# Choosing experts over three tiles in turn, and splitting the first weighted-sum block before the scores end

## The reference, cut to what matters

```python
s = jnp.einsum('thzd,hzkd->thzk', qry, sub_keys)           # t tokens, h 8 heads, z 2 halves, k 128 keys
top_s, top_i = lax.top_k(s, PEER_TOPK)                     # 16 of 128, for each half
cand_s = (top_s[:, :, 0, :, None] + top_s[:, :, 1, None, :]).reshape(nt, PEER_HEADS, kk)
best_s, best_pos = lax.top_k(cand_s, PEER_TOPK)            # 16 of 256 sums
idx = jnp.take_along_axis(cand_i, best_pos, axis=-1)
gate = jax.nn.softmax(best_s, axis=-1)
...
act = jax.nn.gelu(jnp.einsum('td,thkd->thk', tb, expert_u[ib]), approximate=False)
wts = act * gb
out = jnp.einsum('thk,thkd->td', wts, expert_v[ib])
```

## Time and profile before

| | us |
|---|---|
| median of 3 runs (lowest, highest) | 2340.74 (2338.66, 2343.03) |
| the profiled execution | 2343.86 |
| its span, first to last instruction | 2342.0 |
| PE busy in it | 2259.8 (96%) |
| DVE, ACT, POOL busy | 1512.5, 902.6, 1157.2 |

### The profile page before, as it was taken

How to read it: one execution, slowest core, us unless ns; L and a number is a source line. 1 busy time by engine, 2 the same in 40 slices (tenths; PEclk the granted TensorE clock), 3 DMA queues, 4 the chain that set the end, 5 groups by cost and what they waited for, 6 DMA issues and landing times.

```text
span 2342.0 us, 30967 instructions
## 1 busy us (share of the span) xinstructions
PE 2259.8 (96%) x10852; PEld 1879.7 (80%) x10852; DVE 1512.5 (65%) x3525; ACT 902.6 (39%) x1425; POOL 1157.2 (49%) x947
## 2 busy tenths in 40 slices
PE   8999899899989999999999999999989999999998
PEld 6787688788878888888887888888877888888885
DVE  4554666677665354058887888882238888888783
ACT  6454555344334333233333333342223333323342
POOL 3433232766634333315666656665656665555610
PEclk9999999999999999999999999999999999999999
DMA  4222011232344333224444444446458999999940
GB/s 167 90 74 88 19 46 46 93 115 86 134 170 167 111 106 120 72 86 142 149 141 147 136 149 148 148 136 247 146 177 337 387 374 347 362 349 344 364 180 37
DMA packets 160321, 394.71 MB, mean 169 GB/s; under 512 B 27376, under 2 KB 93168, under 8 KB 149872
## 3 DMA queue, kind: packets, MB, share of 16 engines
q1 hardware_dynamic: 125424, 326.32, 40.0%
q0 software_dynamic: 34816, 67.41, 7.8%
HBM read 328.45 MB, written 65.21 MB: 168 GB/s over the span
## 4 chain that ended last, share of the span: by engine, by line
PE 41%; POOL 15%; issue 9%; DVE 2%; DMA 2%; ACT 1%; DVEq 0%; POOLq 0%; SPq 0%
POOL g_dense L1892 14%; PE ps L1329 13%; PE ps L2346 7%; PE ps L2347 7%; PE ps L2348 7%; PE ps L180 2%; PE ps L182 2%; PE ps L181 2%; DMA g_dense<-up_gates_summed_sb,up_gate_at_sb 1%; PE ps L1663 1%; PE ps L2398 1%; DMA expert_rows_sb<-expert_v,chosen_expert_sb 0%; POOL down_picked_gelu_sb L2099 0%; DVE up_spare_sb L1832 0%; DVE up_u_low_sb L1748 0%
## 5 line engine op out<-in xcount | busy, mean ns | idle before, releaser
L1892 POOL DMA_INDIRECT g_dense<-up_gates_summed_sb,up_gate_at_sb x384 | 418.5, 1090 | 308.2 <-issue 232.1
L180 PE MATMUL ps<-n_high_sb,up_u_high_sb 128*128 128x512 f32 x1024 | 398.6, 389 | 0.8 <-issue 0.8
L182 PE MATMUL ps<-n_high_sb,up_u_low_sb 128*128 128x512 f32 x1024 | 398.4, 389 | 0.1
L181 PE MATMUL ps<-n_low_sb,up_u_high_sb 128*128 128x512 f32 x1024 | 398.4, 389 | 0.0
L2346 PE MATMUL ps<-down_v_high_sb,down_w_high_sb 128*128 128x512 f32 x768 | 301.3, 392 | 12.3 <-issue 7.5
L2347 PE MATMUL ps<-down_v_low_sb,down_w_high_sb 128*128 128x512 f32 x768 | 300.8, 392 | 0.0
L2348 PE MATMUL ps<-down_v_high_sb,down_w_low_sb 128*128 128x512 f32 x768 | 300.5, 391 | 0.0
L1748 DVE TENSOR_TENSOR up_u_low_sb<-up_u_sb,up_u_high_sb 128x1024 fp32r<-128x1024 f32 x128 | 156.5, 1223 | 161.5 <-ACT up_u_high_sb L1913 140.9
L2273 ACT ACTIVATE down_v_high_sb<-down_v_sb 128x1024 fp32r<-128x1024 f32 x120 | 126.0, 1050 | 312.1 <-PE ps L2348 289.0
L1925 ACT ACTIVATE up_gelu_sb<-ps 128x512 f32<-128x512 f32 x128 | 76.6, 598 | 398.0 <-PE ps L182 282.5
L180 PEld LDWEIGHTS ps<-n_high_sb,up_u_high_sb 128*128 128x128 f32 x1024 | 192.2, 188 | 42.1 <-issue 2.0
(11 more groups left out here) (347 smaller groups left out, 4687.3 us busy)
## 6 DMA issues: line engine op xcount, KB each, us to landing
up_u_sb<-expert_u SPq DMA_DIRECT2D x128, 512.0 KB
down_v_sb<-expert_v SPq DMA_DIRECT2D x32, 2048.0 KB
a_dense<-up_gelu_sb SPq DMA_DIRECT2D x128, 256.0 KB
g_dense<-nought_sb SPq DMA_DIRECT2D x8, 3072.0 KB, 10.8
down_gelu_sb<-a_dense SPq DMA_DIRECT2D x32, 768.0 KB
down_gates_sb<-g_dense SPq DMA_DIRECT2D x32, 768.0 KB
w_slots_sb<-w_conv SPq DMA_DIRECT2D x19, 1024.0 KB, 4.8
query_slots_sb<-peer_query SPq DMA_DIRECT2D x8, 1024.0 KB, 6.1
```

Of the source, the lines that this page charges most:

```text
L180: pe.matmul(out, ah, bh, start=k == 0, stop=False)
L181: pe.matmul(out, ah, bl, start=False, stop=False)
L182: last = pe.matmul(out, al, bh, start=False, stop=k == n - 1)
L1892: pool.indirect_dma_start(cells, at, summed[:, tt, k:k + 1], None).then_inc(stored[tt], 16)
```

## The change

1. **Order of selection.** `ORDER` goes over the units first and the dense tiles inside: unit 0 of tiles 0, 1 and 2, then unit 1 of each, and so on; tile 3 last, as before. `gates` and `at_f` get a buffer per tile. POOL scatters in that order, with the second head of a unit put one unit later.
2. **Block 0 of the weighted sum.** The value pieces are copied at j = 112 to 115 and their low parts taken one by one from key 116; SP waits for all scatters in step 119 (`GATES_AT`) instead of 124 and loads block 0's gates there, block 1's in step 121; DVE makes the weights after low part 125, ACT copies them at j = 123 and 124, DVE takes their low parts after low part 127.
3. **Block 2.** SP loads its values in step 124 and its gelus and gates in step 126, and block 3 right after the score stage; the loop starts two blocks later.
4. **Rows ahead of picks.** POOL gathers the rows of block 0 when all products are made, and the picks after the `a_dense` stores; from block 1 on the order is as before.

```diff
-    WEIGHTS_AT = PEER_K - 4
-    VALUES_AT = PEER_K - 8
+    VALUES_AT = PEER_K - 16
+    GATES_AT = PEER_K - 9
+    WEIGHED_AT = PEER_K - 3
+    WEIGHTS_AT = PEER_K - 5
     UK = UNIT * TOPK
+    ORDER = [(tt, n) for n in range(UNITS) for tt in range(DENSE)] + [(tt, n) for tt in range(DENSE, TT) for n in range(UNITS)]
...
-        for tt in range(TT):
-            if tt:
+        for c, (tt, n) in enumerate(ORDER):
+            if tt and n == 0:
                 dve.wait_ge(query.out_act, 4 * tt)
...
         for n in range(split[0], PEER_K):
             low_part()
-        dve.wait_ge(low, PEER_K)
-        opening.value_lows(dve)
-        opening.weights(dve)
+            if VALUES_AT + RING <= n < VALUES_AT + RING + DOWN_J - 1:
+                opening.value_low(dve, n - VALUES_AT - RING)
+            if n == PEER_K - RING:
+                dve.wait_ge(low, n + 1)
+                opening.value_low(dve, DOWN_J - 1)
+            if n == WEIGHED_AT:
+                opening.weigh(dve)
+        opening.weight_lows(dve)
...
-            if j == WEIGHTS_AT:
+            if j == GATES_AT:
                 for tt in range(DENSE):
                     sp.wait_ge(stored[tt], 16 * HK)
                 down.load_gates(sp, 0, 0)
+            if j == GATES_AT + 2:
+                down.load_gates(sp, 1, 1)
+            if j == PEER_K - 4:
+                sp.wait_ge(opening.v_low, DOWN_J)
+                down.load_v(sp, 2, 0)
             if j == PEER_K - 2:
-                down.load_gates(sp, 1, 1)
+                sp.wait_ge(opening.w_low, DOWN_J)
+                down.load_gelus(sp, 2, 0)
+                down.load_gates(sp, 2, 0)
...
-        for h in range(5):
-            scatter(0, h)
-        for h in range(3):
-            scatter(0, 5 + h)
-            scatter(1, h)
-        scatter(1, 3)
-        for h in range(4):
-            scatter(1, 4 + h)
-            scatter(2, h)
-        for h in range(4, PEER_H):
-            scatter(2, h)
+        for c in range(DENSE * UNITS):
+            scatter(c, 0)
+            if c < 2:
+                scatter(c, 1)
+            if c > 2:
+                scatter(c - 1, 1)
+        scatter(DENSE * UNITS - 1, 1)
...
-            if j == PEER_K - 2:
+            if j in (WEIGHTS_AT, WEIGHTS_AT + 1):
                 for n in range(DOWN_J // 2):
-                    opening.weight_high(act, n)
+                    opening.weight_high(act, (j - WEIGHTS_AT) * (DOWN_J // 2) + n)
...
-            with sp.Fori(1, NB // 2) as i:
+            sp.wait_ge(w_low, 2 * JB)
+            down.load_gelus(sp, 3, 1)
+            down.load_gates(sp, 3, 1)
+            sp.wait_ge(v_low, 2 * JB)
+            down.load_v(sp, 3, 1)
+            with sp.Fori(2, NB // 2) as i:
...
             pool.wait_ge(up.prod, PEER_K)
+            rows(0)
             for x in up.a_stored:
                 pool.wait_ge(x, up.all_blocks)
-            for n in range(NB):
-                gather(n)
+            picks(0)
+            for n in range(1, NB):
+                picks(n)
+                rows(n)
```

More of the change, by code:

```diff
@@ new lines, in vector @@
+            h0, h1 = n * UNIT, (n + 1) * UNIT
+            ks, gs = slice(h0 * TOPK, h1 * TOPK), slice(h0 * G, h1 * G)
+            for hz in range(2 * h0, 2 * h1):
+                last = top16(scores[:, hz, :], spare[:, hz * PEER_K:(hz + 1) * PEER_K], top_v[:, hz, :], top_i[:, hz, :], 1.7)
+            st.done(last)
+            dve.tensor_copy(top_f[:, 2 * h0:2 * h1, :], top_i[:, 2 * h0:2 * h1, :])
+            tv, tf = (x[:, 2 * h0:2 * h1, :].rearrange("p (h z) k -> p h z k", z=2) for x in (top_v, top_f))
@@ new lines, in vector @@
+            gate = heads(gates_of(tt, n))
+            dve.tensor_tensor(gate, best[:, h0:h1, :], top1, ALU.subtract).then_inc(maxed, 1)
+            exp_at.append(split[0])
+            for z in range(2):
+                if z == 0:
+                    st.done(dve.tensor_scalar(part[:, ks], flat(pos[:, h0:h1, :]), 4, None, ALU.logical_shift_right))
+                else:
+                    st.done(dve.tensor_scalar(part[:, ks], flat(pos[:, h0:h1, :]), 15, None, ALU.bitwise_and))
+                st.done(dve.tensor_copy(part_f[:, ks], part[:, ks]))
+                eq = spare[:, gs].rearrange("p (n a) -> p n a", a=TOPK)
+                st.done(dve.tensor_tensor(eq, part_f[:, ks].unsqueeze(2).broadcast_to([P, UK, TOPK]),
+                                          iota[:, 0:TOPK].unsqueeze(1).broadcast_to([P, UK, TOPK]), ALU.is_equal))
+                st.done(dve.tensor_tensor(grid(spare[:, gs]), grid(spare[:, gs]),
+                                          tf[:, :, z, :].unsqueeze(2).broadcast_to([P, UNIT, TOPK, TOPK]), ALU.mult))
+                st.done(dve.tensor_reduce(chosen[:, z, ks], eq, AX.X, ALU.add))
+                spent(2.8)
@@ new lines, in vector @@
+            spent(1.5)
+            if tt < DENSE:
+                dve.tensor_copy(place[:, tt, ks], at_f[:, ks])
+                for h in range(h0, h1):
+                    before = slice(0, (h + 1) * TOPK)
+                    for q in range(TOPK):
+                        k = h * TOPK + q
+                        last = dve.scalar_tensor_tensor(spare[:, q * HK:q * HK + (h + 1) * TOPK], at_f[:, before], at_f[:, k:k + 1],
+                                                        gates[:, tt, before], ALU.is_equal, ALU.mult, accum_out=summed[:, tt, k:k + 1])
+                        if q % 8 == 7:
+                            spent(2.6)
+                    last.then_inc(placed, 1)
+                    dve.wait_ge(placed, c * UNIT + (h - h0) + 1)
+            else:
+                dve.tensor_copy(m.a_at[:, tt - DENSE, ks], at_f[:, ks])
+                st.done(dve.scalar_tensor_tensor(part_f[:, ks], first, float(PEER_K), second, ALU.mult, ALU.add))
+                dve.tensor_copy(m.v_row[:, tt - DENSE, ks], part_f[:, ks]).then_inc(selected, 1)
@@ L1884, in gpsimd, with scatter @@
     def gpsimd(pool):
-        def scatter(tt, h):
-            pool.wait_ge(placed, tt * PEER_H + h + 1)
+        def scatter(c, half):
+            tt, n = ORDER[c]
+            h = n * UNIT + half
+            pool.wait_ge(placed, c * UNIT + half + 1)
             if h:
@@ L2093, in _, with picks @@
         def _(pool):
-            def gather(n):
+            def picks(n):
                 for u in range(PICK):
@@ L2260, in _ @@
             up.scalar(act)
-            for j in range(JB // 2, JB):
-                opening.weight_high(act, j)
             act.wait_ge(v_in[1], 16)
```

98 lines of the change are left out of this document (30 added, 68 removed).

## The result

| | before | changed |
|---|---|---|
| median (lowest, highest), us | 2340.93 (2338.66, 2343.03) | 2324.97 (2323.33, 2328.43) |
| runs | 4 | 4 |
| the profiled execution | 2343.86 | 2328.43 |
| its span | 2342.0 | 2326.7 |

The changed kernel takes 0.9937 of the time of before, 95% interval 0.9921 to 0.9953: 16.0 us less by the medians, 15.4 by the two profiled executions. The forecast was 2333.4 in a range of 2324 to 2347.

The account below looks back on a forecast made before the run. PE, busy 96% of the span, was taken as the bound. Of 17.6 us winnable in gaps and clock, 8.8 were lost before product 124 and 1.5 at block 2: 7.3 us won, 2333.4 from the median 2340.74, range 2324 to 2347.

Parts of the forecast that it names:

- the gaps at the seam and at block 2: PE idle 7.54 us between scores and weighted sum and 4.72 us before block 2; 17.6 us winnable with the lower clock.
- the scatters that end before 1699.8: Rival, chance 0.10: POOL's transfers get shorter while SP stands still, so the gain is 16 us, time 2324.7.
- 1713.3 - T: The change's total gain in us as a function of the scatters' end, the whole 16 to 17.6 if that is below 1699.8.
- T: End of POOL's scatters, when the memset after them follows; forecast at 1706 us.
- the clock: PE's matmuls run at a lower clock level after a gap; forecast to cost 2.6 us after the idle before product 124.
- (a): Pricing POOL's removed scatter waits one by one: 9 x 2.4 = 21 us, so the memset comes at about 1708.
- (b): Pricing POOL's scatters by heads: 22 x 27.0 + 2 x 29.5 = 653 us, an end at about 1702.
- The rival in which the pauses grow as the waits go: POOL's removed scatter waits return as longer pauses: only 5 us won, scatters end at 1724, time 2351.4; chance 0.15.
- T + 8.5: Start of PE's product 124, behind the delayed load, split and low part: 1714.5, which leaves PE idle 6.2 us.
- no gap before product 124: Sign that the prediction is wrong; it expected PE to be idle there for about 6 us.
- The first gap: PE's idle time between the last score product and the weighted sum, forecast won whole: 9.9 us (7.54 + 2.4).
- The rival in which POOL's gathers wait for DVE: Row gathers wait for DVE's run of subtractions, block 2 is 4.0 + 2.6 us late, time 2338.5; chance 0.13.

Follow-up runs that it names:

- the one trace with 21: The kernel before with its 24 heads scattered tile by tile, so that 21 wait for the head issued right before: 2356.56 us, ratio 1.0058.
- the second copy: The changed kernel measured once more without an edit, beside later kernels: 2327.36 us, ratio to before 0.9944; its profiled execution took 2336.71 us.

## Why the prediction was right, and where it was off

**The direction and the cause held.** The prediction put the gaps at the seam and at block 2 on one chain of scatters. The order alone makes the gain, and without it parts 2 to 4 together win nothing. The size was off: the median, 2324.97, lies 1 us inside the stated range and 3 below the forecast's own range of 2328 to 2341. It is the number of a rival with a chance of 0.10, the scatters that end before 1699.8, 2324.7. In the profiled execution they ended 0.75 us after that. The 1713.3 - T of the sum gives 12.8 for T = 1700.55, and the rest of the 15.4 are the clock, block 2 and 0.2 us of part 2, as told below.

**Part 1.** T was taken as 1706, between (a) 1708 and (b) 1702; it came at 1700.55, and its mean over nine traces is 1701.0. Way (b), by heads, gave 653 us for the 24 heads, and they took 652.2. The mean of the chain over the nine is 651.5. The 2.5 us for a wait holds over the whole range of 2 to 21 waits, though not evenly: 3.1 for each of the first nine, 2.0 for each of the last ten. The rival in which the pauses grow as the waits go is refuted both ways: "issue" has a mean of 225 us with 2 waits and of 227 with 11, and 232.8 in the one trace with 21.

**Part 2.** The term of T + 8.5 for the start of product 124 came out at T + 8.27 (1708.82 - 1700.55), and at T + 8.1 to 8.3 in four further traces: at T = 1701.94, 1702.26 and 1703.78 with the new order, where PE stood for 3.8 to 4.2 us, and at 1723.62 with the old one, where it stood for 25. So the price of the load behind the wait was right. The idle time was 3.3 us instead of 6.2, since T was 5.5 us earlier, the term 0.2 shorter, and PE reached product 124 2.8 us earlier than in the trace that 1708.3 was taken from. Of those, 2.1 are pauses of PE in that trace near 1234 us, which the changed kernel's trace doesn't have, and 0.5 an earlier start of the scores. The clock took 1.7 us, not 2.6: that price had been taken from rows after longer gaps, of 7.5 and 4.7 us. The prediction named one sign that it was wrong, no gap before product 124, which did come in the second copy's trace; there PE was later than the load, as shown above.

**Part 3.** The first gap was won whole, as forecast.

**Part 4.** Block 2 was forecast to cost 1.5 us; it cost nothing, but narrowly. DVE's last low part of block 2 in the changed kernel:

```profile
1764.16 0.54 DVE L2161 TENSOR_TENSOR down_w_low_sb<-down_gelu_sb,down_w_high_sb 128x384 fp32r<-128x384 f32 x1
```

It ended 32.4 us after the start of the weighted sum, and PE needed it after 32.65: the forecast's bounds were 28 and 35. (144 x 0.2267 is 32.6, not the 32.8 of the forecast.) The rival in which POOL's gathers wait for DVE gave that block 2 is late by 4 us; it isn't. Of POOL's first eight gathers the four that were issued while DVE subtracted (1735.34 to 1740.15) took 1.29 to 1.31 us, and the four before and after them 0.95 to 0.98. So DVE's run of subtractions cost each of them 0.3 us, less than one of DVE's instructions, and never the whole run. The Trainium skill's page "SBUF — State Buffer", section "SBUF: two separate sides", on which this rival drew, speaks of one instruction, and these rows are within that; the rival had stretched it to a whole run. The first pick of 8 us in three other traces, which does look like a whole run, is open (below).

**The sum.** Forecast 7.3 us, measured 15.4 between the profiled executions. Product 124 was forecast for T + 8.5 = 1714.5 and started at 1708.82, 5.7 us earlier, of which T makes 5.5. The clock took 0.9 less than forecast and block 2 1.5 less. These make 8.1, the whole difference. PE's pauses in the trace of before don't enter it, since its end hung on T and not on PE. By the medians the gain was 16.0. So the mechanism was right, and **the term that was mis-sized most is T**: 1706 was a compromise between two ways of pricing, and the way by heads was the right one. That it hit within 1.5 us in this execution is in part luck, since T spread over 14 us in nine traces.

**What the sum left out** is what part 1 does by itself. The prediction took the 8.8 us of part 2 as the price for winning the first gap. But with T at 1706 SP comes to step 124 at 1712.6 (the kernel with the order alone), after the scatters' end; the gates need no earlier place, and the last gelu on ACT is no longer behind them. Rows of before that say so: ACT's copies had waited for the gates' product, and the gelu stood behind them. My expectation for the order alone, 8 us too high, failed for the same reason.

## What to carry to other kernels

Before pricing the parts of a change one by one, ask of each what it does alone: two gaps of one engine, 40 us apart, can hang on one late chain through the order of instructions on a third engine, and one of the edits then wins nearly all of it (15 of 16 us here). Moving a wait forward in a queue of transfers is free only as long as what it waits for is early; when it is late, it now stops everything that the queue still has to load (2351 instead of 2325 us here). And of a chain of transfers that sets the end one trace gives the length only to some 8 to 15 us.

## What the runs showed that was not expected

- The length of the scatter chain differs from execution to execution, by 8 us in four traces of the old order (674.4 to 682.6) and by 15 in nine of the new one. Where it sets the end, the times spread: before took 2324.75 to 2350.85 us in the 66 runs of the three later comparisons, so its fastest run was as fast as the changed kernel's median, and one tile after another took 2349.2 to 2363.8 in 8. The changed kernel's first four runs lie within 5.1 us, but its second set of 11 spreads over 12.3 us, for which the one trace shows pauses of PE in the middle of the scores and a start 3 us later; the cause of those is open.
- The first pick took 8.02, 8.03 and 8.02 us in the three traces with a late chain and the picks first (before twice, and tile by tile), within a run of DVE's products and subtractions without a pause. In all three it ended 0.85 to 0.86 us after the run's last subtraction, as if it had waited for the whole run. But in the kernel with the order alone it was issued in the midst of such a run, too, and took 1.32 us, and behind a late chain with the rows first it took 1.20. What makes the difference was not found, and no kernel was made to tell it.
- The row gathers of block 0 took 12.1 us from POOL's issue to DVE's use behind the early loads of blocks 2 and 3, and 8.6 in the kernel that differs by them alone: transfers that are started early for one block can make another block's late.
